# Up-projection of a decoder layer: three 256 column matmuls per weight tile in place of a 512 and a 256 column one

## The reference

```python
h = rms_norm(x, g_ffn[l])
u = h @ w_up[l]                                  # 2048 -> 11264: 5632 gate and 5632 value columns
up = jnp.pad(u, ((0, 0), (CONV_WIDTH - 1, 0), (0, 0)))
conv = sum(wc[t] * up[:, t:t + s] for t in range(CONV_WIDTH)) + b_conv[l]
gate, val = jnp.split(conv, 2, axis=-1)
x = x + (jax.nn.silu(gate) * val) @ w_down[l]    # 5632 -> 2048
```

## Time and profile before

| what | value |
|---|---|
| median of three runs | 1414.11 us |
| the profiled execution: its span, from the first to the last instruction | 1413.1 us |
| the median above that span | 1.0 us |
| TensorE matmuls busy, number | 1405.8 us, 6947 |
| TensorE weight loads busy | 1184.9 us |
| VectorE busy | 890.7 us |
| ScalarE busy | 722.2 us |
| granted TensorE clock over the span, mean | 1.000 |

### The profile page before, as it was taken

The page is one execution under the profiler, slowest core; times in us unless marked ns, Lnnn a source line. Parts: engine busy times, 40 slices in busy tenths (PEclk is TensorE's granted clock), DMA queues, the critical chain, the costliest instruction groups (busy, mean ns, idle before and its releaser), DMA issues.

```text
span 1413.1 us, 19396 instructions
## 1 busy us (share of the span) xinstructions
PE 1405.8 (99%) x6947; PEld 1184.9 (84%) x6947; DVE 890.7 (63%) x1109; ACT 722.2 (51%) x884; POOL 53.0 (4%) x65
## 2 busy tenths in 40 slices
PE   8999999999999999999999999999999999999999
PEld 7888888888888888888888888888888888888887
DVE  5646455655454456555577767676767676776765
ACT  6655444464545444444555554555454645554551
POOL 0112111110000000000000000000000000000000
PEclk9999999999999999999999999999999999999999
DMA  9865555556666655756566666666666665656652
GB/s 332 257 188 162 160 160 167 170 165 189 181 188 183 189 188 187 239 182 194 176 194 182 198 185 187 190 189 189 188 185 193 179 195 176 203 170 206 178 191 93
DMA packets 138441, 265.97 MB, mean 188 GB/s; under 512 B 10528, under 2 KB 10784, under 8 KB 137888
## 3 DMA queue, kind: packets, MB, share of 16 engines
q1 hardware_dynamic: 135488, 262.36, 60.7%
q10 hardware_dynamic: 2912, 3.06, 0.7%
HBM read 263.29 MB, written 2.10 MB: 188 GB/s over the span
## 4 chain that ended last, share of the span: by engine, by line
PE 99%; DMA 0%; DVE 0%; SPq 0%; ACT 0%; issue 0%
PE acc L327 22%; PE acc L307 20%; PE acc L309 20%; PE acc L308 20%; PE acc L324 12%; PE acc L323 1%; PE acc L348 0%; PE acc L336 0%; PE acc L359 0%; PE acc L375 0%; DMA raw<-w_in 0%; PE acc L368 0%; PE acc L437 0%; PE acc L376 0%; PE acc L356 0%; PE acc L362 0%
## 5 line engine op out<-in xcount | busy, mean ns | idle before, releaser
L815 DVE TENSOR_TENSOR w_lo<-raw,w_hi 128x1024 fp32r<-128x1024 f32 x487 | 593.7, 1224 | 466.5 <-ACT w_hi L568 463.6
L568 ACT ACTIVATE w_hi<-raw 128x1024 fp32r<-128x1024 f32 x487 | 513.5, 1058 | 558.9 <-PE acc L309 372.6
L327 PE MATMUL acc<-actB,w_hi 128*128 128x512 f32 x1320 | 466.9, 398 | 0.0
L307 PE MATMUL acc<-w_hi,actA 128*128 128x512 f32 x1116 | 442.3, 396 | 2.0 <-DVE w_lo L815 2.0
L309 PE MATMUL acc<-w_hi,actA 128*128 128x512 f32 x1116 | 435.1, 390 | 0.0
L308 PE MATMUL acc<-w_lo,actA 128*128 128x512 f32 x1116 | 434.4, 389 | 0.0
L324 PE MATMUL acc<-actB,w_lo 128*128 128x256 f32 x1408 | 391.9, 281 | 0.0
L327 PEld LDWEIGHTS acc<-actB,w_hi 128*128 128x128 f32 x1320 | 248.0, 188 | 60.4
L324 PEld LDWEIGHTS acc<-actB,w_lo 128*128 128x128 f32 x1408 | 265.9, 189 | 2.0
L309 PEld LDWEIGHTS acc<-w_hi,actA 128*128 128x128 f32 x1116 | 209.5, 188 | 44.4
L307 PEld LDWEIGHTS acc<-w_hi,actA 128*128 128x128 f32 x1116 | 209.7, 188 | 43.7 <-issue 2.4
(11 more groups left out here) (141 smaller groups left out, 591.6 us busy)
## 6 DMA issues: line engine op xcount, KB each, us to landing
raw<-w_up SPq DMA_DIRECT2D x176, 512.0 KB, 4.2
raw<-w_in SPq DMA_DIRECT2D x159, 512.0 KB, 3.9
raw<-w_down SPq DMA_DIRECT2D x88, 512.0 KB, 4.5
raw<-w_out SPq DMA_DIRECT2D x32, 512.0 KB, 4.5
raw<-w_fox SPq DMA_DIRECT2D x16, 512.0 KB, 4.5
raw<-w_dil SPq DMA_DIRECT2D x16, 512.0 KB, 4.5
work<-x_t SPq DMA_DIRECT2D x8, 256.0 KB, 6.7
work<-x SPq DMA_DIRECT2D x2, 1024.0 KB, 8.9
```

The costliest lines, as they stand in the source:

```text
L307: nc.tensor.matmul(o, lhsT=a_h, rhs=w_hi[:, u, k, :], start=first and k == 0, stop=False)
L327: mm = nc.tensor.matmul(banks[j][:, :], lhsT=hi_w, rhs=actB[:, kt, :], start=False, stop=kt == KT - 1)
L568: nc.scalar.activation(w_hi[:, u, :, :], raw[:, u % RAW_SLOTS, :].rearrange("p (k n) -> p k n", k=KU), ACT.Copy).then_inc(hi_done, 1)
L815: nc.vector.tensor_tensor(w_lo[:, u, :, :], raw[:, u % RAW_SLOTS, :].rearrange("p (k n) -> p k n", k=KU), w_hi[:, u, :, :].bitcast(f32), A ...
```

## The change

`cols_unit` gets a pair of banks in place of four. Column tile j has one half of a bank: half j % 2 of bank j // 2. All three products of a weight tile are matmuls of 256 columns, one behind the other into the same 256 columns of PSUM: high weights by high activations, low weights by high activations, high weights by low activations. Only the first matmul in each bank carries the start flag. The sum is then complete in PSUM. `low_copy` and the add are gone; VectorE waits for the round's last matmul itself and scales the two banks in one instruction into `upad`. TensorE's waits on `up_added` become waits on `u_ready`, the scaling's semaphore. ScalarE's waits that guarded `tmp_j` go with the copy.

```diff
-            def cols_unit(R, u, banks):
+            def cols_unit(R, u, pair):
                 pe.wait_ge(lo_done, UPR * R + u)
                 for k in range(KU):
                     kt = KU * u + k
+                    a_h, a_l = actB[:, kt, 0:SEQ], actB[:, kt, SEQ:2 * SEQ]
                     for j in range(CT):
                         hi_w, lo_w = w_hi[:, u, k, j * P:(j + 1) * P], w_lo[:, u, k, j * P:(j + 1) * P]
-                        if kt == 0:
-                            nc.tensor.matmul(banks[j][:, :], lhsT=hi_w, rhs=actB[:, kt, :], start=True, stop=False)
-                        mm = nc.tensor.matmul(banks[j][:, SEQ:], lhsT=lo_w, rhs=actB[:, kt, 0:SEQ],
-                                              start=False, stop=False)
-                        if kt > 0:
-                            mm = nc.tensor.matmul(banks[j][:, :], lhsT=hi_w, rhs=actB[:, kt, :], start=False,
-                                                  stop=kt == KT - 1)
+                        o = pair[j // 2][:, (j % 2) * SEQ:(j % 2 + 1) * SEQ]
+                        nc.tensor.matmul(o, lhsT=hi_w, rhs=a_h, start=kt == 0 and j % 2 == 0, stop=False,
+                                         skip_group_check=True)
+                        nc.tensor.matmul(o, lhsT=lo_w, rhs=a_h, start=False, stop=False, skip_group_check=True)
+                        mm = nc.tensor.matmul(o, lhsT=hi_w, rhs=a_l, start=False, stop=kt == KT - 1,
+                                              skip_group_check=True)
                 mm.then_inc(used, 1)
...
-                up_round(FF0 + 1 + 3 * i, bank[0:4])
+                up_round(FF0 + 1 + 3 * i, bank[0:2])
                 pe.wait_ge(d_added, 1 + 8 * i)
-                up_round(FF0 + 2 + 3 * i, bank[4:8])
+                up_round(FF0 + 2 + 3 * i, bank[4:6])
                 pe.wait_ge(a_lo, i + 1)
-                pe.wait_ge(up_added, 2 * i + 2)
+                pe.wait_ge(u_ready, 2 * i + 2)
...
-            def low_copy(R, q, b0):
-                act.wait_ge(used, UPR * R + UPR)
-                nc.scalar.activation(tmp_j, acc[:, b0:b0 + CT, SEQ:2 * SEQ], ACT.Copy).then_inc(low_copied, 1)
...
-            def add_up(q, b0):
-                dve.wait_ge(low_copied, q + 1)
-                nc.vector.tensor_tensor(tmp_j, acc[:, b0:b0 + CT, 0:SEQ], tmp_j, ALU.add).then_inc(up_added, 1)
-                dve.wait_ge(up_added, q + 1)
-                nc.vector.tensor_tensor(upad[:, :, 2:2 + SEQ], tmp_j,
+            def scale_up(R, q, b0):
+                dve.wait_ge(used, UPR * R + UPR)
+                nc.vector.tensor_tensor(upad[:, :, 2:2 + SEQ],
+                                        acc[:, b0:b0 + 2, :].rearrange("p b (j s) -> p (b j) s", j=2),
                                         rstd_row.rearrange("p (a s) -> p a s", a=1).broadcast_to([P, CT, SEQ]),
                                         ALU.mult).then_inc(u_ready, 1)
```

More of the change, by code:

```diff
@@ L205, in decoder_layer @@
         diag_ready, bc_ready, bc_done = sem("diag_ready"), sem("bc_ready"), sem("bc_done")
-        low_copied, up_added, u_ready, tap2, conv_done, silu_done = (
-            sem("low_copied"), sem("up_added"), sem("u_ready"), sem("tap2"), sem("conv_done"), sem("silu_done"))
+        u_ready, tap2, conv_done, silu_done = sem("u_ready"), sem("tap2"), sem("conv_done"), sem("silu_done")
         a_ready, a_hi, a_lo, d_added = sem("a_ready"), sem("a_hi"), sem("a_lo"), sem("d_added")
@@ L510, in _ @@
                     pe.wait_ge(x2t_lo, 16)
-                cols_unit(FF0, u, bank[4:8])
+                cols_unit(FF0, u, bank[4:6])
                 if u == 2:
@@ L520, in _, with up_round @@
             pe.wait_ge(bc_done, 1)
-            def up_round(R, banks):
+            def up_round(R, pair):
                 for u in range(UPR):
-                    cols_unit(R, u, banks)
+                    cols_unit(R, u, pair)
             def down_unit(R, u, first_kt, first_bank, row0=None):
@@ L531, in _ @@
             with pe.Fori(0, BLOCKS - 2) as i:
-                up_round(FF0 + 1 + 3 * i, bank[0:4])
+                up_round(FF0 + 1 + 3 * i, bank[0:2])
                 pe.wait_ge(d_added, 1 + 8 * i)
-                up_round(FF0 + 2 + 3 * i, bank[4:8])
+                up_round(FF0 + 2 + 3 * i, bank[4:6])
                 pe.wait_ge(a_lo, i + 1)
-                pe.wait_ge(up_added, 2 * i + 2)
+                pe.wait_ge(u_ready, 2 * i + 2)
                 for u in range(UPR):
                     if u == 4:
-                        pe.wait_ge(up_added, 2 * i + 3)
+                        pe.wait_ge(u_ready, 2 * i + 3)
                     if u == 6:
@@ L542, in _ @@
                     down_unit(FF0 + 3 + 3 * i, u, 0, 0)
-            up_round(V_PREV, bank[0:4])
+            up_round(V_PREV, bank[0:2])
             pe.wait_ge(d_added, 1 + 8 * (BLOCKS - 2))
-            up_round(G_LAST, bank[4:8])
-            pe.wait_ge(up_added, 2 * BLOCKS - 2)
-            up_round(V_LAST, bank[0:4])
+            up_round(G_LAST, bank[4:6])
+            pe.wait_ge(u_ready, 2 * BLOCKS - 2)
+            up_round(V_LAST, bank[0:2])
             pe.wait_ge(a_lo, BLOCKS - 1)
-            pe.wait_ge(up_added, 2 * BLOCKS - 1)
+            pe.wait_ge(u_ready, 2 * BLOCKS - 1)
             for u in range(UPR):
                 if u == 4:
-                    pe.wait_ge(up_added, 2 * BLOCKS)
+                    pe.wait_ge(u_ready, 2 * BLOCKS)
                 down_unit(D_PREV, u, 0, 4)
@@ L771, in _ @@
                     nc.scalar.activation(rstd_row, bank[2][:, 0:SEQ], ACT.Copy).then_inc(bc_done, 1)
-            low_copy(FF0, 0, 4)
             def value_round(V, i):
@@ L780, in value_round @@
                         gate_silu(2 * i)
-                act.wait_ge(u_ready, 2 * i + 1)
-                low_copy(V, 2 * i + 1, 0)
             def gate_round(G, i):
@@ L790, in gate_round @@
                         hidden_high(i)
-                act.wait_ge(a_lo, i + 1)
-                low_copy(G, 2 * i + 2, 4)
             with act.Fori(0, BLOCKS - 2) as i:
@@ L1089, in _ @@
             dve.wait_ge(bc_done, 1)
-            add_up(0, 4)
+            scale_up(FF0, 0, 4)
             def value_round(V, i):
@@ L1096, in value_round @@
                         older_taps(2 * i, 4 * i)
-                add_up(2 * i + 1, 0)
+                scale_up(V, 2 * i + 1, 0)
             def gate_round(G, i):
@@ L1107, in gate_round @@
                         hidden_low(i)
-                add_up(2 * i + 2, 4)
+                scale_up(G, 2 * i + 2, 4)
             with dve.Fori(0, BLOCKS - 2) as i:
```

## The result

The changed kernel takes 1426.3 us (median of four runs, 1425.25 to 1427.11), the kernel before 1414.36 us beside it. The ratio is 1.0081, with a 95% interval of 1.0067 to 1.0095: slower by 11.9 us, where 1412.6 was forecast and the range ended at 1425. The profiled execution has a span of 1424.8 us and a time of 1426.59.

A forecast was written before the change was run, and what follows sets the result against it. The prediction took TensorE's streaming of matmuls to bound the kernel: -1.5 us for the up-projection's matmuls, 0 elsewhere, so 1414.1 - 1.5 = 1412.6 us, with an 8 in 10 range of 1395 to 1425.

The forecast's parts named there:

- What bounds the kernel: Whole kernel: it ends when TensorE, busy 99% of the 1413.1 us span, has streamed its matmuls.
- ScalarE and VectorE, the waits on PSUM, the tail: Copy and add go, 49 us of engine time, PSUM waits move to the scaling, end unchanged: each 0 us.
- The pace of 256 column matmuls in a row: Up-projection on TensorE: 0.1173 us each, 495.5 us over 1408 tiles against 497.0 before, -1.5 us.
- rival B: Up-projection: short matmuls too short for their own weight load; at 0.120 us each +9.9 us, 1424.0; chance 0.33.
- Half of a long matmul for a short one: Up-projection tile: unstalled 0.2267 + 0.1133 = 0.340 us, leaving 0.013 us of each loop tile as stall.
- rival A: Up-projection: equal matmuls run without stall, like down rounds; -18.3 us in full, -8.8 for half; chance 0.35.
- The eight transposes: Transposes of 128 columns with own loads, next matmul 0.79 us after the first: about 0.1 us a pair.
- The range: Total time: 8 in 10 range of 1395 to 1425 us.
- The fixed cost of 2.5 ns a matmul: Up-projection: 1408 more matmuls would cost 3.5 us by the skill page; set aside as not borne out by the trace.

The follow-up runs named there:

- The relief alone: Kernel before without ScalarE's copy and VectorE's add, VectorE scaling the banks' lower halves, TensorE's matmuls unchanged: 1414.85 us against 1414.36, ratio 1.0004.
- the runs of 8: Kernel before with each up-projection unit's eight 512 column matmuls first, then its eight 256 column ones: 1410.01 us against 1414.55, ratio 0.9966.
- The bench: No kernel: TensorE alone, 26 stretches of 96 matmuls of varied lengths; with 128 moving columns, starts 111.7 ns apart for 128 stationary columns, 85.0 for 96.

## Why the prediction was wrong

*What bounds the kernel*: right. The chain is TensorE before and after, no wait was added, and the count of columns, instructions and rounds held.

*ScalarE and VectorE, the waits on PSUM, the tail*: right, each at 0. The relief alone gives 1.0004. The scaling takes 1217 ns as taken, in the place where it was put.

*The pace of 256 column matmuls in a row*: this step failed. I took 0.1173 us, a mean over gaps between long matmuls with one pair among them, and leaned away from 0.120, the longest gap in the rows. But a short matmul behind a long one is not a sample of short ones in a row. The first short one of that pair starts at 786.29 and takes 0.11; the second, the only one behind a short one, takes 0.12:

```profile
786.40 0.28 PE L324 MATMUL acc<-actB,w_lo 128*128 128x256 f32 x1
786.52 0.40 PE L327 MATMUL acc<-actB,w_hi 128*128 128x512 f32 x1
```

In the 22 such pairs of the trace of before the second takes 118 to 120 ns. In a row each takes 0.1200 in this kernel, so the term is 506.9 us and not 495.5: 11.4 of the 13.7 us of error. It is rival B's pace, at the price worked out for it (1424.0). Its chance, 0.33, was as high as the forecast's 0.32, and nothing in the working favoured the middle but that it lay between.

*Half of a long matmul for a short one*: the mistake under it. "Unstalled" was put at 0.2267 + 0.1133, which takes the fixed cost of a matmul for nothing, and a fixed cost was set aside because 0.23 and 0.11 look like a half. They are (227 and 113 ns), but 113 is what the first short one behind a long one takes, in the runs of 8 too, where the next take 119 and 120. In a row it is 226.7 and 120.0, and 13.3 ns of each are fixed. By this reading the change adds 1408 x 13.3 ns = 18.8 us and takes away the stall of the alternation, 6.7 ns on 1344 tiles, 9.0 us: +9.8, against the +9.9 of the rows. For the 1056 more matmuls of the halved down rounds the same rule gives 14.1 us, where 14.2 were measured.

*The argument for rival A*: half right. The stall did go with the alternation, 9.0 us, which is A's price for half of the stall (8.8); the fixed costs of 1408 more matmuls took twice as much. Down rounds are fast because their matmuls are long, not because they are equal; cut in halves they run at 0.1200 too.

*B's mechanism*: not shown. The prediction set its point at a load of over 0.1177 us. The load takes 0.1117, less than that, and it binds only up to 240 moving columns. The eight transposes held against B were also misread: 0.79 us over eight is 0.1, but the trace has seven distances of 108 to 110 ns and one of 28 or 29 before the next matmul. What the 13.3 ns are, why they are 20.0 at 448 columns, and why they change with the load's size and with 64 bytes of place, no run here shows, and it stays open.

*The range*: its upper end was the upper bound of this one term, with nothing for the rest. The remaining 2.3 us are about what the profiled execution shows beside it: the later start of the up-projection (1.3 us, with the clock at its lower level in the start-up), the time outside the span (1.8 us for the 1.0 carried over) and the down rounds (0.3).

*The fixed cost of 2.5 ns a matmul* (the Trainium skill, "TensorE: Matmul & The Clock Gate", "Back-to-back issue gap", which has it on top of the columns over 2.4 GHz) was set aside wrongly. The form fits what was measured here in f32r with 128 stationary columns, the size does not: 0.4167 ns a column is 2.4 GHz, and the fixed part is 13.3 ns at 256, 320, 352, 384 and 512 columns. The section "LDWEIGHTS (loading the stationary operand)" of that page puts a load at its columns over 1.2 GHz, 107 ns for 128. The bench's 111.7 and 85.0 ns for 128 and 96 columns agree in slope and lie 5 ns above it; for 64 columns no run shows the load by itself.

## What to carry to other kernels

Where each matmul brings its own weight load of 128 columns in this number form, count 120 ns for 256 moving columns and 226.7 for 512, not half of the one for the other, and give every load 512 columns where the layout allows: two matmuls of 256 cost 13.3 ns more than one of 512. Going below 256 saves little: 128 to 240 columns all take 111.7 ns. A price per column is to be read from two lengths, not from one. Where long and short matmuls must both be, put each kind in runs; here that made 6.9 us by order alone. A gap is to be read from a stretch with the same neighbours as the new code will have; where only a single pair has them, its second member is the sample, not the mean over the others.

## What the runs showed of the hardware

- In f32r at the upper clock level, with a load of 128 columns for each matmul, 256, 320, 352, 384 and 512 moving columns take 120.0, 146.7, 160.0, 173.3 and 226.7 ns: 0.4167 ns a column and 13.3 ns over. At the lower level 512 take 427 ns, 0.833 a column (twice 0.4167) and nothing over.
- 128 to 240 moving columns take 111.7 ns whatever their number, where a load of 96 columns gives 85.0 with 128 moving; at the lower level 64 moving columns take 213 ns.
- Other lengths leave the line: 448 take 206.7 ns, 6.7 above it, 480 take 216.7, 3.4 above it, 272 and 288 lie 1.4 and 1.6 below it.
- A smaller load speeds a short matmul and slows a long one: with 64 stationary columns 256 take 113.3 for 120.0 and 512 take 230.1 for 226.7.
- A shift of one operand by 64 bytes changes the pace: 256 in a row from 120.0 to 117.8, 512 in a row from 226.7 to between 228.9 and 233.4.
- 512 and 256 in turn run in repeating patterns (236, 113, 233, 117, 241, 120), the same with all other engines quiet, and in at least two of them, 353.3 and 347 ns a pair. In runs of their own the two take 346.7, and each pair of runs costs 20 ns.
